# Expert outputs summed into the residual rows in memory, one expert after another, in a decoder layer with 32 experts

## The reference

```
xn2   = rms_norm(x2, norm_ffn)
experts, gates = router(xn2)                  # two experts and two gates a token
h     = silu(xn2[tok] @ w_gate[e]) * (xn2[tok] @ w_up[e])
y[tok] += gates[tok, k] * (h @ w_down[e])     # for the tokens of expert e
out   = rms_norm(x2 + y, norm_final)
```

## Time and profile before

| | |
|---|---|
| median of 3 runs | 1862.19 us (1859.02 to 1863.63) |
| the profiled execution: its time, its span | 1859.37 us, 1857.5 us |
| PE busy | 1789.4 us (96%) |
| DVE busy | 1143.4 us (62%) |
| ACT busy | 862.8 us (46%) |
| POOL busy | 481.9 us (26%) |
| DMA | 333.18 MB, mean 179 GB/s |
| chain that ended last | 36% PE; DVE 2%, DMA 2% |

### The profile page before, as it was taken

How to read it: one execution, slowest core, us unless ns; L and a number is a source line. 1 busy time by engine, 2 the same in 40 slices (tenths; PEclk the granted TensorE clock), 3 DMA queues, 4 the chain that set the end, 5 groups by cost and what they waited for, 6 DMA issues and landing times. The chain is left out here.

```text
span 1857.5 us, 29133 instructions
## 1 busy us (share of the span) xinstructions
PE 1789.4 (96%) x9988; PEld 1535.9 (83%) x9988; DVE 1143.4 (62%) x1913; ACT 862.8 (46%) x1540; POOL 481.9 (26%) x491
## 2 busy tenths in 40 slices
PE   7989999999999999999998999969999999999997
PEld 5878888999999878788888988857888888888883
DVE  4256676311111254545446456679999999999985
ACT  4245555411111223222223223348878778788873
POOL 3013222000000132313231112232965433333220
PEclk9999999999999999999999999979999999999998
DMA  7112211232212303020203553269999999999987
GB/s 215 61 32 57 58 46 47 69 92 80 68 58 77 93 23 94 23 93 23 94 1 103 166 182 103 98 231 391 392 385 385 385 383 387 384 386 392 386 344 291
DMA packets 176955, 333.18 MB, mean 179 GB/s; under 512 B 36704, under 2 KB 105856, under 8 KB 175792
## 3 DMA queue, kind: packets, MB, share of 16 engines
q1 hardware_dynamic: 154912, 278.07, 41.6%
q0 software_dynamic: 21296, 53.26, 8.3%
q10 hardware_dynamic: 672, 0.85, 0.3%
HBM read 304.11 MB, written 46.35 MB: 189 GB/s over the span
## 5 line engine op out<-in xcount | busy, mean ns | idle before, releaser
L2719 POOL DMA_INDIRECT y_d<-e_y,e_idxs x32 | 134.3, 4196 | 203.2 <-DVE e_y L2823 188.1
L2794 DVE TENSOR_TENSOR e_Lg<-e_rawg,e_Hg 128x1024 fp32r<-128x1024 f32 x128 | 148.4, 1223 | 6.4 <-ACT e_Hg L2743 6.3
L2794 DVE TENSOR_TENSOR e_Lu<-e_rawu,e_Hu 128x1024 fp32r<-128x1024 f32 x128 | 148.1, 1225 | 0.0
L2794 DVE TENSOR_TENSOR e_Ld<-e_rawd,e_Hd 128x1024 fp32r<-128x1024 f32 x124 | 143.6, 1227 | 0.0
L2743 ACT ACTIVATE e_Hg<-e_rawg 128x1024 fp32r<-128x1024 f32 x128 | 125.1, 1050 | 8.0 <-DMA e_rawg<-in_w_gate 8.0
L2743 ACT ACTIVATE e_Hd<-e_rawd 128x1024 fp32r<-128x1024 f32 x124 | 122.4, 1051 | 3.2 <-DMA e_rawd<-in_w_down 2.9
L152 PE MATMUL bank<-r_wH,xH 128*128 128x512 f32 (+1 forms) x288 | 119.3, 414 | 3.4 <-DVE r_stacked L1571 3.4
L2743 ACT ACTIVATE e_Hu<-e_rawu 128x1024 fp32r<-128x1024 f32 x124 | 120.9, 1059 | 0.0
L154 PE MATMUL bank<-r_wH,xL 128*128 128x512 f32 (+1 forms) x288 | 113.9, 396 | 0.0
L153 PE MATMUL bank<-r_wL,xH 128*128 128x512 f32 (+1 forms) x288 | 113.5, 394 | 0.0
L152 PE MATMUL bank<-e_Hg,e_xH 128*128 128x512 f32 x256 | 100.7, 393 | 3.1 <-DVE e_xL L2800 3.1
(11 more groups left out here) (435 smaller groups left out, 4753.7 us busy)
## 6 DMA issues: line engine op xcount, KB each, us to landing
e_rawg<-in_w_gate SPq DMA_DIRECT2D x128, 512.0 KB
e_rawu<-in_w_up SPq DMA_DIRECT2D x128, 512.0 KB
e_rawd<-in_w_down SPq DMA_DIRECT2D x124, 512.0 KB
raw<-in_w_in SPq DMA_DIRECT2D x51, 512.0 KB, 4.2
c_Y<-y_d SPq DMA_DIRECT2D x8, 1024.0 KB, 13.0
m_t<-b_m_s POOLq DMA_DIRECT2D x8, 528.0 KB
m_gate<-gate_t POOLq DMA_DIRECT2D x8, 528.0 KB, 4.1
m_m<-m_t POOLq DMA_DIRECT2D x8, 528.0 KB, 3.9
```

The lines of the kernel that those rows point to most:

```text
L2719: pool.indirect_dma_start(out=ch.y_d, out_offset=bass.IndirectOffsetOnAxis(ap=idx[:, e % IDX, 1:2], axis=0), in_=y[:], in_offset=None, bou ...
L2794: dve.tensor_tensor(L[kind][:, q], raw[kind][:, q], H[kind][:, q].bitcast(F32), ALU.subtract).then_inc(w_lo[kind], 1)
```

## The change

The buffer `y_d` goes. The gates are stored to a new buffer `gates_d` (one value for each pair) at the start of the loop. For each expert POOL gathers the gates of its list into `gate` and the current residual rows `x2_d` of its tokens into `acc`, both single buffers. `out_evac` multiplies by the gate on both engines. DVE adds its half of `acc` in the same instruction; POOL adds the other half (`tensor_tensor`, 128x512) before it scatters, and the scatter now goes back to `x2_d` by the token's index. Since two experts can have the same token, the gather of `acc` for expert e waits until the scatter of e-1 has landed (`y_st`). `Beyond` is changed likewise. `Combine` loads one row a token from `x2_d`, squares, and scales; PE, the diagonals and the early loads of the residual rows are no longer used there.

```diff
@@ output_programs
             pool.wait_ge(mm_done, NT)
-            pool.memset(ch.e_rows[:], 0.0).then_inc(ch.e_go, 1)
+            for t in (ch.e_rows, ch.e_acc, ch.e_gate):
+                pool.memset(t[:], 0.0).then_inc(ch.e_go, 1)
             fill(NT - 2)
...
-            pool.wait_ge(ch.e_go, 1)
+            pool.wait_ge(ch.e_go, 3)
             expert_gather(pool, ch, 0)
...
-                done(dve.tensor_tensor(ch.gates[0:m, t, 1:2], ch.gates[0:m, t, 0:1], den[0:m, 1:2], ALU.mult))
+                dve.tensor_tensor(ch.gates[0:m, t, 1:2], ch.gates[0:m, t, 0:1], den[0:m, 1:2], ALU.mult).then_inc(ch.gates_done, 1)
@@ class Combine
     def sync(self, sp):
         ch = self.ch
         self.served(sp)
         for t in self.ORDER:
             m = rows_of(t)
-            sp.dma_start(self.Y[0:m, t], ch.y_d[2 * t * P:2 * (t * P + m), :].rearrange("(p k) d -> p k d", k=2)).then_inc(self.y_in[t], 16)
+            sp.dma_start(self.X[0:m, t], ch.x2_d[t * P:t * P + m, :]).then_inc(self.x_in[t], 16)
...
+            act.wait_ge(self.x_in[t], 16)
+            if n:
+                act.wait_ge(self.sq_done, n)
+            act.activation(self.junk[0:m], self.X[0:m, t], ACT.Square, accum_out=stat[0:m, t, 0:1]).then_inc(self.sq_done, 1)
...
+            dve.scalar_tensor_tensor(out=X[0:m, t], in0=X[0:m, t], scalar=stat[0:m, t, 3:4], in1=gain[0:m], op0=ALU.mult, op1=ALU.mult).then_inc(self.o_done, 1)
@@ stage_experts, SP
-                for t in range(NT):
-                    m = rows_of(t)
-                    sp.dma_start(ch.x2_tiles[0:m, t], ch.x2_d[t * P:t * P + m, :]).then_inc(ch.x2_in, 16)
@@ stage_experts, POOL
+                def store_gates():
+                    pool.wait_ge(ch.gates_done, NT)
+                    pool.dma_start(ch.gates_d[0:2 * SEQ, :].rearrange("(t p k) o -> p t (k o)", t=NB, k=2), ch.gates[:, 0:NB, :]).then_inc(gates_st, 16)
+                    pool.dma_start(ch.gates_d[2 * SEQ:, :].rearrange("(p k) o -> p (k o)", k=2), ch.gates[0:NS, NB, :]).then_inc(gates_st, 16)
+                    pool.wait_ge(gates_st, 32)
+
+                def sums_so_far(e):
+                    pool.indirect_dma_start(out=gate[:], out_offset=None, in_=ch.gates_d,
+                                            in_offset=bass.IndirectOffsetOnAxis(ap=idx[:, e % IDX, 1:2], axis=0),
+                                            bounds_check=2 * T - 1, oob_is_err=False).then_inc(gate_in, 16)
+                    if e:
+                        pool.wait_ge(y_st, e * 16)
+                    pool.indirect_dma_start(out=acc[:], out_offset=None, in_=ch.x2_d,
+                                            in_offset=bass.IndirectOffsetOnAxis(ap=idx[:, e % IDX, 0:1], axis=0),
+                                            bounds_check=T - 1, oob_is_err=False).then_inc(acc_in, 16)
+
                 def scatter(e):
                     pool.wait_ge(y_a, e + 1)
+                    pool.wait_ge(acc_in, e * 16 + 16)
+                    pool.tensor_tensor(y[:, 0:512], y[:, 0:512], acc[:, 0:512], ALU.add).then_inc(y_sum, 1)
+                    pool.wait_ge(y_sum, e + 1)
                     pool.wait_ge(y_b, e + 1)
-                    pool.indirect_dma_start(out=ch.y_d, out_offset=bass.IndirectOffsetOnAxis(ap=idx[:, e % IDX, 1:2], axis=0),
-                                            in_=y[:], in_offset=None, bounds_check=2 * T - 1, oob_is_err=False).then_inc(y_st, 16)
+                    pool.indirect_dma_start(out=ch.x2_d, out_offset=bass.IndirectOffsetOnAxis(ap=idx[:, e % IDX, 0:1], axis=0),
+                                            in_=y[:], in_offset=None, bounds_check=T - 1, oob_is_err=False).then_inc(y_st, 16)
...
                     if e >= 1:
                         scatter(e - 1)
+                    else:
+                        store_gates()
+                    sums_so_far(e)
                     if 2 <= e < 2 + NT:
                         fill_beyond(e - 2)
@@ stage_experts, ACT
                 def out_evac(e):
...
-                    act.activation(y[:, 0:512], Y[0][:], ACT.Copy).then_inc(y_a, 1)
+                    act.wait_ge(gate_in, e * 16 + 16)
+                    act.activation(y[:, 0:512], Y[0][:], ACT.Copy, scale=gate[:, 0:1]).then_inc(y_a, 1)
...
-                combine.diagonals(act)
@@ stage_experts, DVE
                 def out_evac(e):
...
-                    dve.tensor_copy(y[:, 512:1024], Y[1][:]).then_inc(y_b, 1)
+                    dve.wait_ge(gate_in, e * 16 + 16)
+                    dve.wait_ge(acc_in, e * 16 + 16)
+                    dve.scalar_tensor_tensor(out=y[:, 512:1024], in0=Y[1][:], scalar=gate[:, 0:1], in1=acc[:, 512:1024],
+                                             op0=ALU.mult, op1=ALU.add).then_inc(y_b, 1)
@@ stage_experts, PE
                 beyond.tensor(pe)
-                pe.wait_ge(y_a, NE)
-                pe.wait_ge(y_b, NE)
-                combine.tensor(pe)
```

More of the change, by code:

```diff
@@ L2418, in gpsimd @@
         pool.memset(idx[:], 0).then_inc(self.go, 1)
-        pool.memset(rows[:], 0.0).then_inc(self.go, 1)
-        pool.wait_ge(self.go, 2)
+        for t in (rows, self.gate, self.acc):
+            pool.memset(t[:], 0.0).then_inc(self.go, 1)
+        pool.wait_ge(self.go, 4)
         self.each(pool, body)
@@ L2436, in body @@
             act.wait_ge(self.y_st, j * 16)
+            act.wait_ge(self.gate_in, j * 16 + 16)
             for f in range(2):
-                ins = act.activation(self.y[:, f * 512:(f + 1) * 512], banks[5 + f][:], ACT.Copy)
+                ins = act.activation(self.y[:, f * 512:(f + 1) * 512], banks[5 + f][:], ACT.Copy, scale=self.gate[:, 0:1])
             ins.then_inc(self.y_out, 1)
@@ L2515, in sync @@
             dst = ch.y_sample if t == NB else ch.y_prompt[t * P:(t + 1) * P, :]
-            sp.dma_start(dst, self.Y[0:m, t, 0]).then_inc(self.o_st, 16)
+            sp.dma_start(dst, self.X[0:m, t]).then_inc(self.o_st, 16)
         sp.wait_ge(self.o_st, 16 * NT)
-    def diagonals(self, act):
-        for i, t in enumerate(self.ON_PE):
-            m = rows_of(t)
-            for k in range(2):
-                act.activation(self.diag[0:m, i, k, 0:m], self.ch.ident[0:m, 0:m], ACT.Copy, scale=self.ch.gates[0:m, t, k:k + 1]).then_inc(self.diag_done, 1)
     def scalar(self, act):
-        stat, pe_tiles, order = self.stat, list(self.ON_PE), self.ORDER
+        stat, order = self.stat, self.ORDER
         def square(n):
@@ L2552, in scalar @@
         square(0)
-        for t in range(NT):
-            if t + 1 < NT:
-                square(t + 1)
-            root(t)
+        for n in range(NT):
+            if n + 1 < NT:
+                square(n + 1)
+            root(n)
     def vector(self, dve):
-        Y, x2, stat, gates, gain = self.Y, self.ch.x2_tiles, self.stat, self.ch.gates, self.gain
-        pe_tiles, order = list(self.ON_PE), self.ORDER
-        def weigh(t):
-            i = self.ON_DVE.index(t)
-            dve.wait_ge(self.y_in[t], 16)
-            dve.scalar_tensor_tensor(out=Y[:, t, 0], in0=Y[:, t, 0], scalar=gates[:, t, 0:1], in1=x2[:, t], op0=ALU.mult, op1=ALU.add).then_inc(self.half, 1)
-            dve.wait_ge(self.half, i + 1)
-            dve.scalar_tensor_tensor(out=Y[:, t, 1], in0=Y[:, t, 1], scalar=gates[:, t, 1:2], in1=Y[:, t, 0], op0=ALU.mult, op1=ALU.add).then_inc(self.a_done, 1)
+        X, stat, gain, order = self.X, self.stat, self.gain, self.ORDER
         def mean(n):
@@ L2640, in stage_experts @@
         sem("e_sig"), sem("e_mul"), sem("e_h"), sem("e_ht"), sem("e_hhi"), sem("e_hlo"), sem("e_ya"), sem("e_yb"))
+    gates_st, gate_in, acc_in, y_sum = sem("e_gst"), sem("e_gin"), sem("e_accin"), sem("e_ysum")
+    gate, acc = ch.e_gate, ch.e_acc
     with ExitStack() as st:
@@ L2960, in hybrid_decoder_layer @@
     ch.toktab = nc.dram_tensor("toktab", [SLOTS, 2], I32).ap()
-    ch.y_d = nc.dram_tensor("y_d", [2 * T, D], F32).ap()
+    ch.gates_d = nc.dram_tensor("gates_d", [2 * T, 1], F32).ap()
     with ExitStack() as top:
```

93 lines of the change are left out of this document (24 added, 69 removed).

## The result

The changed kernel takes **1894.99 us** (median of 4 runs, 1892.54 to 1898.06). The kernel before, run beside it on the same chip, takes 1862.91 us (1859.02 to 1865.15). The ratio is 1.0192, 95% interval 1.0175 to 1.021: slower by 32 us.

A forecast was written before the change was run, and what follows sets the result against it. PE was taken to set the period of 17.72 us an expert, with DMA and DVE near their limits. Plain intervals 30 + fill intervals 48 + last interval 2 + last scatter 1 - end 12 = +69 on 1859.4: 1928 us, range 1880 to 1990.

The forecast's parts named there:

- what the end gives: Behind the last scatter: fewer bytes loaded, so 25.2 us in place of 36.9, a gain of 12 us.
- "+2" for the last interval: Last expert interval: add, scatter, landing and gather in series take some 9.7 us, today 7.7, so +2.
- "+1.2" for the last scatter: End of the loop: the last scatter stands behind an add, +1.2 us.
- DMA needs 17.84 + 0.7 + 0.1 = 18.7: Expert loop: loads need 17.84 us an expert, gathered rows add 0.70, the gates' tiny packets 0.1.
- rival A: Expert loop: DMA alone binds, the chain fits under 18.7 us; +23, 1882 us; chance 0.12.
- The larger term is a new closed chain: Expert loop: add, scatter, landing, next gather and its landing set 19.2 us a plain interval; twenty intervals cost 30 us.
- DVE's `Ld` run of 4.6 begins then and holds the scatter: 6.6: Chain in the loop: POOL's scatter waits for DVE's run and ends 6.6 us after `acc_in`.
- Two intervals take 46.0 us: Iterations 2 to 10: `fill_beyond` crowds POOL's queue, 23.0 us an interval, 5.3 over today's; nine cost 48 us.
- Together 0.4 against 0.26 us of idle ... PE's lead hides it: DVE in the loop: `e_y` and POOL's add cost 0.4 us; the drift of 0.14 us an expert is hidden.
- 0 for both: Before and at the loop's start: memsets of `e_acc` and `e_gate`, and storing the gates, cost 0.
- Rival B: Whole kernel: all loop additions are hidden and the tail's gain stays; -11, 1848 us; chance 0.10.
- Rival C: Loop: PE's clock falls, or POOL never finds gaps; intervals 21 to 28 us, 1977 us at 22; chance 0.08.

The follow-up runs named there:

- kernel 3: The changed kernel without the `acc` gather and both additions, with the gates kept: 1853.12 us, ratio 0.9955 to the kernel before.
- kernel 2: The changed kernel with the `acc` gather reading rows that nobody writes and not waiting for the scatter: 1887.43 us, ratio 1.0153 to the kernel before.
- kernel 5: The changed kernel without POOL's addition, its waits, all DMAs and DVE's half kept: 1890.17 us, ratio 1.016 to the kernel before.
- kernel 8: kernel 1 with one POOL addition ahead of each scatter, into a tile nobody reads: 1855.88 us, ratio 0.9976 to the kernel before.
- kernel 7: The changed kernel loading 768 of 1024 columns of each weight chunk from expert 2 on: 1862.29 us, ratio 1.0024 to the kernel before.
- kernel 6: The changed kernel without the 18 indirect DMAs of `fill_beyond`: 1889.94 us, ratio 1.0172 to the kernel before.
- kernel 10: The changed kernel with the edits of kernel 2 and kernel 6 together: 1887.03 us, ratio 1.0161 to the kernel before.
- Kernel 11: The changed kernel without the store of the gates and without their gather: 1888.42 us, ratio 1.0163 to the kernel before.
- kernel 4: The changed kernel with a scatter that adds in the DMA replacing the sums' gather and both additions: 1885.68 us, ratio 1.0145 to the kernel before.
- kernel 1: The changed kernel with the expert loop of before, so the changed final step alone: 1846.15 us, ratio 0.9923 to the kernel before.

## Why the prediction was right or wrong

**What bounds the kernel before, and what the end gives: right.** 24.8 us behind the last landing for a forecast of 25.2. The transfers fill it as forecast: from 1875 to 1894 the DMA share was 1.02, at 400 GB/s. But DVE isn't "inside of it": its scale by row and gain follows itself nine times, in the chain that ended last, until 1889.8, and the last store goes out behind it. No run tells which of the two binds there. (The "1.7" for that store comes out of its own rows as 2.7 less 1.3, so 1.4.)

```profile
1871.43 3.82 DMA c_X<-x_d
1875.27 1.16 ACT c_junk L2529 x2
...
1878.30 1.28 DVE c_X L2559
...
1879.84 1.28 DVE c_X L2559
```

**"+2" for the last interval and "+1.2" for the last scatter: right as a sum.** Three landings now follow each other at the end of the loop: scatter, `acc`, scatter, and again (the same chain, 1843.30 to 1871.04):

```profile
1843.30 7.05 DMA x_d<-e_y,e_idxs
1851.11 4.09 DMA e_accs<-x_d,e_idxs
1855.34 1.27 POOL e_y L2672
1857.40 3.24 DMA x_d<-e_y,e_idxs
1861.40 4.20 DMA e_accs<-x_d,e_idxs
1867.80 3.23 DMA x_d<-e_y,e_idxs
```

From expert 31's sigmoid (1844.24) to that last landing it takes 26.8 us, before 23.1 (1797.50 to 1820.6): +3.7 for a forecast +3.2; the interval from expert 30 to 31 is 2.1 shorter.

**"DMA needs 17.84 + 0.7 + 0.1 = 18.7": the term of 0.7 was mis-sized.** The gates' 0.1 measured 0.12 (kernel 3). The gather's 0.27 MB at 386 GB/s measured 1.21 us in place of 0.70 (kernel 2 less kernel 3; POOL's addition, which differs too, is worth 0.14 at most, kernel 5). This bound is 19.2, and it is rival A's mechanism that holds in the late stretch, at a dearer price. I had priced the rows at the rate of a queue that carries 92% weights; with the added rows the rate itself falls, from 386 to 376 GB/s over the late stretch. Why the engines give less with them isn't shown. The Trainium skill (DMA: Bandwidth & Descriptors, Anatomy of one DMA) gives about 2.0 us and bytes over 436 GB/s for one DMA from GpSimd; the same gather landed 7.5 us after its issue here and cost the loop 1.21, so the measurement decides against it in full queues.

**"The larger term is a new closed chain", 19.7 or 17.8: wrong late, and one step of it failed.** That step is "DVE's `Ld` run of 4.6 begins then and holds the scatter: 6.6". POOL around the scatter of 1766.71:

```profile
1764.63 1.28 POOL L2672 TENSOR_TENSOR e_y<-e_y,e_accs 128x512 f32<-128x512 f32 x1 [4.63 <-DMA e_accs<-x_d,e_idxs]
1766.71 1.17 POOL L2675 DMA_INDIRECT x_d<-e_y,e_idxs  x1 [0.80 <-POOL e_y L2672]
1768.18 1.98 POOL L2660 DMA_INDIRECT e_gates<-gates_d,e_idxs  x1 [0.30 <-issue]
1775.09 1.00 POOL L2665 DMA_INDIRECT e_accs<-x_d,e_idxs  x1 [4.92 <-DMA x_d<-e_y,e_idxs]
1782.69 1.95 POOL L2672 TENSOR_TENSOR e_y<-e_y,e_accs 128x512 f32<-128x512 f32 x1 [4.66 <-DMA e_accs<-x_d,e_idxs]
```

The scatter is issued 3.25 us after the start of the add and not 6.6; it lands at 10.5 (forecast 8.8 to 11.8, a slower landing having eaten what the quicker issue gave); the gates are past by 5.5 and not 12.0; `acc` is issued by 11.5 (13.3) and the next add starts at 18.06. Thus the chain takes 18.1 us. Experts 12 to 15 come at that pace (18.12), before the loop falls to the loads' 19.21; the likely reason is a lead that the loads won while the chain and the fills held the loop back. That the chain sets the 18.12 isn't shown, since kernel 8, which has no chain, takes 18.12 there as well, by DVE. Most of the signs that I had named for "right" came out (19 to 20 us an expert late, DVE waiting for `acc`, a DMA share below 1 early), and they fitted a chain that didn't bind: the loads had to be told from it by kernels 2 and 7.

**"Two intervals take 46.0 us", 48 us for nine: wrong by 28 us, and nearly all of the miss.** It is the same step, and here it compounds. The early part of the loop on POOL, one whole interval:

```profile
1344.59 1.34 POOL L2672 TENSOR_TENSOR e_y<-e_y,e_accs 128x512 f32<-128x512 f32 x1
1346.72 1.17 POOL L2675 DMA_INDIRECT x_d<-e_y,e_idxs  x1 [0.79 <-POOL e_y L2672]
1348.20 1.02 POOL L2660 DMA_INDIRECT e_gates<-gates_d,e_idxs  x1 [0.31 <-issue]
1355.17 1.00 POOL L2665 DMA_INDIRECT e_accs<-x_d,e_idxs  x1 [5.95 <-DMA x_d<-e_y,e_idxs]
1356.48 4.63 POOL L2650 DMA_INDIRECT toktab<-tokens,slots  x1 [0.30 <-issue]
1361.41 0.99 POOL L2650 DMA_INDIRECT toktab<-tokens,slots  x1 [0.30 <-issue]
1363.31 2.07 POOL L2339 DMA_INDIRECT e_rowss<-xn_d,e_idxs  x1 [0.30 <-issue]
1365.40 1.34 POOL L2672 TENSOR_TENSOR e_y<-e_y,e_accs 128x512 f32<-128x512 f32 x1
```

The order is the one forecast: `acc`, the first fill caught by a run (4.63), the second in the gap (0.99), the row gather, the add with no wait of its own. But the fills end at 17.8 (20.5), the row gather at 20.8 (26), and the next scatter isn't caught either. 20.8 us follow 20.8, where I had 26 and then a scatter 6.6 behind. Of the 2.26 us over today's, 1.5 are the loads and 0.7 this queue (kernels 2, 6, 10).

What the queue holds back is PE's next rows. Between 1310 and 1480 PE waited for the row gather 6 times, 14.2 us in all; in kernels 2, 6 and 10 it did so not once. The wait behind the gather of 1363.31, and PE's clock then (columns as above):

```profile
1371.90 1.96 PE L2842 MATMUL bank<-identity,e_rowss 128*128 128x128 f32 x8 [3.03 <-DMA e_rowss<-xn_d,e_idxs]
...
1372.00:1374.00 2.00, 2.00 (x9) 2.00 (x10) 2.00 (x2) 0.69 (x2) 0.00 (x0) 0.50 1.06 359
```

**"Together 0.4 against 0.26 us of idle ... PE's lead hides it": wrong, though hidden here.** DVE's bound with POOL's addition is 18.00 us (kernel 8), 0.28 over PE's 17.72; over the whole loop it costs 9.7 us. In the changed kernel the loads' 19.2 lies above it.

**"0 for both" (storing the gates): wrong by some 3 us.** POOL waits for the store, and ACT's `y` for the gates behind it:

```profile
1273.34 2.94 POOL L2660 DMA_INDIRECT e_gates<-gates_d,e_idxs  x1 [10.99 <-DMA gates_d<-gates]
...
1281.63 0.69 ACT L2722 ACTIVATE e_y<-bank,e_gates 128x512 f32<-128x512 f32 x1 [3.81 <-DMA e_gates<-gates_d,e_idxs]
```

The cover that I named was there for POOL; what stood behind it, the first `y`, was not looked at. Kernel 11 gives 3.2 us of it back between experts 1 and 3, though its median comes only 2 us closer to the kernel before in all.

**Rival B** (all hidden) failed at the loads: with 19.2 us of them no landing time could have saved it. **Rival C** shows in part, early: after PE had stood still for 3 us its granted clock was 0.50, the 1.2 GHz level, from 1371.9 to 1377.5 (the rows above), that interval took 23.7 us, and over experts 3 to 12 the clock was 0.96 for 1.00 in kernels 2, 6 and 10. Late it was 1.00, the 2.4 GHz level. How much of the 0.7 us above the loads is the clock isn't separated; in kernel 4, with 0.96 there too, the early stretch takes 19.07 for 19.01 late.

Found from both sides, then: the end gives 13.8 us (kernel 1), and the loop takes back 46, of which the gather of the sums accounts for most: without the sums it is 1853.12 us (kernel 3), 7 us under before. No version that computes the full output (the changed kernel, kernel 4 and, for these inputs, kernel 6) beats the kernel before, which reads 8.65 MB of `y_d` rows behind the loop, at 414 GB/s in 21 us; the 8.65 MB of sums gathered in the loop, with their additions, cost 1887.43 - 1853.12 = 34 us (kernel 2 less kernel 3).

## What to carry to other kernels

Before a step is put into a loop, write down what each resource needs per round and by how little it is hidden: here the loads already needed 17.84 of 17.72 us, so every added byte was paid in full and above the average rate. A long row of waits on an idle engine is not a bound: take the wait away and leave its transfers (kernel 2), then take bytes away and leave the wait (kernel 7); the two together name the bound. And a hold that one row shows (the scatter's 4.57 us) can belong to that row's neighbours and not to the operation (1.17 us in kernel 8, 1.13 in kernel 5); a chain in which it is counted again and again multiplies the error.

## What the runs showed of the hardware that was not expected

- An indirect DMA that POOL issues into a gapless run of DVE's two-input splits took 4.57 us, yet with a POOL addition ahead of it, even 4.8 us ahead, it took 1.17, with nothing else changed (means 1151 ns and 4309 ns, kernels 8 and 1). In kernel 5 it took 1.13 without an addition. Why isn't shown.
- POOL's addition of 128x512 took between 1.25 and 5.75 us (kernel 8), and cost a DVE run up to 1.11 us (5.72 for 4.61), three times the 0.35 estimated from one tiny operation.
- 0.27 MB of gathered rows cost 1.21 us where the DMA share was 0.99 to 1.00 (0.70 at the mean rate); halving the bytes at the same count of rows took 0.7 of it.
- With an adding scatter POOL's queue took 11.0% of the engines' time for 5.01 MB, with a plain one 8.5% for 5.68 MB (kernels 4 and 3).
- PE stood still for 3.03 us early in the changed kernel, and its granted clock was 0.50 for the 5.6 us behind it.
- Storing 2112 gates of 4 bytes kept POOL waiting for 10.99 us.
